# Two gated layers on one Trainium2 core: a sixth gate and up pair as seven block products, and an earlier panel split on ScalarE

## The reference, cut to what matters

```python
def _swiglu(h, w_in, w_out):
    gate, up = jnp.split(h @ w_in, 2, axis=-1)
    return (jax.nn.silu(gate) * up) @ w_out

x = x + _swiglu(_rmsnorm(x, norm2[i]), w_ffn_in[i], w_ffn_out[i])   # i = 0, 1
```

## Time and profile before

| what | value |
|---|---|
| median of 3 runs | 2103.74 us (2103.64 to 2107.66) |
| the profiled execution | 2107.25 us |
| its span in the profile | 2105.5 us, 40321 instructions |
| TensorE busy | 2025.5 us (96%) |
| VectorE busy | 1462.1 us (69%) |
| ScalarE busy | 946.5 us (45%) |
| GpSimd busy | 289.1 us (14%) |
| mean granted TensorE clock | 0.993 |
| DMA | 173.89 MB, mean 83 GB/s |

### The profile page before, as it was taken

The page is one execution under the profiler, slowest core; times in us unless marked ns, Lnnn a source line. Parts: engine busy times, 40 slices in busy tenths (PEclk is TensorE's granted clock), DMA queues, the critical chain, the costliest instruction groups (busy, mean ns, idle before and its releaser), DMA issues. The chain is left out here.

```text
span 2105.5 us, 40321 instructions
## 1 busy us (share of the span) xinstructions
PE 2025.5 (96%) x17186; PEld 1280.6 (61%) x17186; DVE 1462.1 (69%) x2207; ACT 946.5 (45%) x1459; POOL 289.1 (14%) x344
## 2 busy tenths in 40 slices
PE   7999999999999999999999999999998999999998
PEld 3657554565588444888745665885565445445766
DVE  4776764888799468765458887986746475786774
ACT  4335765433354674423244433645345345332433
POOL 2621331000001010222110000111012102000000
PEclk9999999999999999999999999999999999999999
DMA  6452003333434311010033333443410022332331
GB/s 159 129 146 56 2 2 87 94 102 99 115 102 123 101 61 60 16 51 4 3 89 90 103 105 110 129 118 101 139 62 21 21 81 60 101 100 65 116 116 65
DMA packets 259224, 173.89 MB, mean 83 GB/s; under 512 B 22528, under 2 KB 254148, under 8 KB 259044
## 3 DMA queue, kind: packets, MB, share of 16 engines
q1 hardware_dynamic: 258138, 170.35, 27.7%
q10 hardware_dynamic: 906, 0.96, 0.2%
HBM read 169.18 MB, written 2.10 MB: 81 GB/s over the span
## 5 line engine op out<-in xcount | busy, mean ns | idle before, releaser
L2718 DVE TENSOR_TENSOR w_lo<-wring,w_hi 128x2048 bf16<-128x2048 f32 (+5 forms) x258 | 440.4, 1718 | 180.6 <-ACT w_hi L2050 179.4
L1312 PE MATMUL banks<-arena,w_hi 128*128 128x512 bf16 (+3 forms) x1840 | 531.6, 372 | 6.4 <-issue 3.5
L2050 ACT ACTIVATE w_hi<-wring 128x2048 f16<-128x2048 f32 (+5 forms) x258 | 366.2, 1431 | 319.9 <-DVE wring L2711 150.0
L1312 PE MATMUL banks<-arena,w_lo 128*128 128x512 f16 (+1 forms) x920 | 342.4, 372 | 0.0
L1312 PEld LDWEIGHTS banks<-arena,w_hi 128*128 128x128 f16 x1840 | 179.8, 98 | 211.6 <-issue 10.6
L1388 PE MATMUL banks<-arena,w_hi 128*128 128x256 f16 (+1 forms) x1848 | 303.4, 273 | 4.3 <-ACT rcol L2099 2.7
L1388 PE MATMUL banks<-arena,w_lo 128*128 128x256 f16 x924 | 251.9, 273 | 0.0
L1150 POOL TENSOR_TENSOR arena<-arena,ntmp 128x512 f32<-128x512 f32 (+1 forms) x72 | 93.2, 1294 | 1108.4 <-ACT ntmp L2080 1102.4
L1312 PE MATMUL banks<-h_hi,w_hi 128*128 128x512 f16 (+1 forms) x536 | 204.0, 381 | 5.1 <-DVE w_lo L2718 5.1
L1312 PE MATMUL banks<-h_hi,w_lo 128*128 128x512 f16 (+1 forms) x536 | 203.9, 380 | 0.0
L1312 PE MATMUL banks<-h_lo,w_hi 128*128 128x512 bf16 (+1 forms) x536 | 203.7, 380 | 0.0
(11 more groups left out here) (479 smaller groups left out, 3395.5 us busy)
## 6 DMA issues: line engine op xcount, KB each, us to landing
wring<-in_w_ffn_in SPq DMA_DIRECT2D x68, 512.0 KB, 5.1
wring<-in_w_ffn_out SPq DMA_DIRECT2D x64, 256.0 KB, 4.0
wring<-in_w_ff SPq DMA_DIRECT2D x16, 1024.0 KB, 5.4
wring<-in_rw_w_in SPq DMA_DIRECT2D x11, 1024.0 KB, 5.3
wring<-in_w_in SPq DMA_DIRECT2D x11, 1024.0 KB, 5.2
wring<-in_w_ffn_in SPq DMA_DIRECT2D x40, 256.0 KB, 3.8
wring<-in_w_ff SPq DMA_DIRECT2D x32, 256.0 KB, 3.8
wring<-in_nsa_w_in SPq DMA_DIRECT2D x7, 1024.0 KB, 6.6
```

The costliest lines, as they stand in the source:

```text
L1312: last = mm(v, p[0], p[1], start=(i == 0), stop=(i == len(prods) - 1))
L2050: A(hi, raw, ACT.Copy).then_inc(split_hi, 1)
L2718: V.tensor_tensor(lo_, raw, hi, ALU.subtract).then_inc(split_lo, 1)
```

## The change

A sixth job of each gated layer, number 20, the 21st, becomes a block. TensorE, at the end of the job loop, waits for the last evacuation of the layer's blocks (all their second tiles), since what follows may use banks 4 to 7. ScalarE, in a job that is followed by a block (4, 7, 10, 13, 16, 19), makes the high halves up to the `split_ahead` of that block before the Silu of the job; that adds one panel, the plain one behind the block. VectorE's program order has no such edit.

```diff
-BLOCKED = (5, 8, 11, 14, 17)
+BLOCKED = (5, 8, 11, 14, 17, 20)
...
                     products(u_[0], u_[1])
+                read_out(pe, [st["ts"][1] for _, _, _, st, _ in jobs if st is not None])
                 if f is ffn[1]:
                     arrived(mem2_panel)
...
-                for g_, u_, e_, st, w in jobs:
+                for n, (g_, u_, e_, st, w) in enumerate(jobs):
                     t = g_[0]
                     split_to(split_ahead(w))
                     if st is not None:
...
                         A(term_t[:, 0:4:3, :], sets(bank[4]), ACT.Copy).then_inc(first_copied, 1)
+                    if e_ + 1 in BLOCKED:
+                        split_to(split_ahead(jobs[n + 1][4]))
                     act.wait_ge(evac_v, t.order + 1)
                     A(gate_b[e_ % 2], gate_b[e_ % 2], ACT.Silu).then_inc(silued, 1)
```

## The result

The changed kernel takes a median of **2112.52 us** (2110.98 to 2115.31, 6 runs); the kernel before, beside it on the same chip, 2103.51 (2102.17 to 2107.66, 6 runs). The ratio is 1.0041, with a 95% interval of 1.0030 to 1.0051: 9.0 us slower by the medians, 6.3 to 10.7 by the interval. The profiled execution of after took 2112.33 us, close to its median.

A forecast was written before the change was run, and what follows sets the result against it. TensorE was taken to bound the kernel, busy 2025.5 us, 96% of the span. 2 x 3.6 - 1.16 + 1.5 = +7.5 us on the median of 2103.74 gave 2111.2 us; range 2104.5 to 2115.

The forecast's parts named there:

- The block itself: TensorE's gated jobs: a block replaces a plain pair, -1.19 us per layer; the added wait behind the job loop costs nothing.
- The early split: ScalarE splits ahead of Silu, so TensorE's gap behind block 5 goes: -0.58 us per layer, -1.16 in all.
- the cover at odd jobs: Job 13: Silu's delay is hidden because VectorE waits for block 14 until 502.92 anyway, with 0.8 us to spare.
- What the block pushes: VectorE behind block 20: up 21 starts at +15.4 us, the second pair panel 14.5 behind job 21's products, before 9.73.
- +3.6 per layer: Second pair panel in the first layer, 1338.94 us in the second: +4.8 late less the block's 1.19, each layer.
- The clock: TensorE behind the first layer's second pair panel gap: slow stretch, +1.5 us; in the second layer nearly free.
- Rival 2: Slow stretches count in both layers, as second-layer splits wait for units TensorE reads late: +1.5 more, 2112.7 us; chance 0.1.
- rival 1: No slow clock behind either layer's gap: +6.0, 2109.8 us; chance 0.2.
- Rival 3: VectorE catches up, second pair panel's low half ready by 583.2: -3.5, 2100.2 us; chance 0.17.
- Rival 4: Early split delays Silu at odd jobs beyond its cover, blocks slip while VectorE catches up: 2104.4 us; chance 0.08.
- The sum: Whole kernel: 2 x 3.6 - 1.16 + 1.5 = +7.5 us; 2114.8 against the profiled execution, 2111.2 against the median.

The follow-up runs named there:

- the run with 18 filling products: Changed kernel plus 18 unused products of ones by ones ahead of the first layer's second pair panel wait: 2110.57 us, ratio 1.0026.
- the block alone: Changed kernel without ScalarE's early split, all six blocks kept: 2113.93 us, ratio 1.0045.
- the split alone: Changed kernel without the block at job 20, so five blocks with the early split: 2102.64 us, ratio 0.9985.
- the late sums: Changed kernel with the first pair panel's sums and their halves moved behind the pair's mixing in job 21: 2107.93 us, ratio 1.0016.
- the sixth block at 19: Changed kernel with blocks at 5, 8, 11, 13, 16 and 19, early split kept: 2101.64 us, ratio 0.9982.
- eight blocks: Changed kernel with blocks at every odd job from 5 to 19, early split kept: 2095.07 us, ratio 0.9956.
- seven blocks: Changed kernel with blocks at 5, 7, 9, 11, 13, 16 and 19, early split kept: 2097.59 us, ratio 0.9964.
- eight without the early split: Changed kernel with blocks at every odd job from 5 to 19 and ScalarE's early split removed: 2133.93 us, ratio 1.0141.

## Why the prediction was right

It forecast 2111.2 us and slower; measured were 2112.5 and slower. Step by step, in the prediction's order:

- **The block itself, 9.17 us and free read-out wait:** as predicted. No gap stands at 574.35.
- **The early split, -0.58 per layer:** the gap behind block 5 is gone in both layers. The term was set too small: the gap costs 0.70 per layer and not 0.58, since TensorE loses another 0.1 us before block 8, so -1.4 where -1.16 was counted. Alone, the split moves the root of the second layer from 1338.94 to 1337.37, by 1.57 us, of which 0.2 stand already at the start of block 5 (404.21, before 404.39), and the medians by 1.6. Of the cover at odd jobs, 0.8 us by the prediction, enough was left: TensorE has no gap in the gated jobs.
- **What the block pushes:** behind block 20 the next split of ScalarE starts at +4.60 (predicted 4.61), the plain unit's low half ends its wait and starts at +6.10 (6.12), up 21 at +15.37 (15.4), the second pair panel at +24.89, 14.53 behind job 21's products (14.5). TensorE's gap is 4.59 (near 4.9), gate 21 takes 0.43. The borrowed rows of block 14, an even block too, gave each of these within 0.1 us.
- **+3.6 per layer:** with the -0.58 the prediction has +3.0 per layer; the account shows -0.7 - 1.2 + 4.8 = +2.9 in the first and +2.9 in the second.
- **The clock, +1.5:** the stretch behind the first gap was at 0.70 and cost 1.67 us by the run with 18 filling products. In the second layer it was at 0.50, costlier for the products, and was absorbed before the root, as predicted: the chain took 34.22 us and not more. Rival 2 falls by this row, rival 1 by the first stretch. The size of the term owes something to luck all the same: the block alone, with the same gap of 4.58 in the first layer, had 0.50 and not 0.70 there, and the 1.00 behind the gap of 2.71 in the earlier trace rows, the prediction's only row for a gap of that length, was the exception among the kernels profiled (last section). The Trainium skill ("TensorE: Matmul & The Clock Gate", Part 1: The HAM clock gate) says that the throttled state is the default and activity releases it. The trace agrees, in a dense part of the kernel too: 0.70 and 0.50 behind gaps of 4.59 and 4.42.
- **Rival 3**, that VectorE catches up by 583.2: the low half ended at 588.7. **Rival 4**, that the early split slips blocks: the split alone is not slower.
- **The sum, +7.5:** the account up to the root of the second layer gives 8.5 - 1.0 = +7.5. The medians give +9.0, with 6.3 to 10.7 in the interval; 1.5 us are left, which these runs do not tell from the scatter between executions. The expected place of the remainder, a clock that differs from one execution to the next, is shown below in several kernels, but is not shown to be the cause of these 1.5. That the sum meets the trace to 0.1 us is in part luck: the split's term was 0.2 too small and the clock's 0.2 too small, and they have opposite signs.

One thing was set too loosely. The sum against the profiled execution (2114.8) and that against the median (2111.2) lay 3.6 us apart, and the prediction chose the median without saying why. The reason could have been looked for in the trace: the low clock between 1620 and 1640 us, worth 3.3 us, stands there and has nothing to do with the gated layers.

The added wait at the end of TensorE's job loop was not taken out in a run, as TensorE could then write a bank that is still being read; that it costs nothing rests on the trace alone.

## What to carry to other kernels

When work is made cheaper on the engine that bounds the kernel, follow the same edit through the queues of its feeders, up to the first chain without slack: here 1.19 us saved in products next to such a chain made it start 4.8 late in each layer, and with the last block one job earlier nothing was lost. An operation that waits for another engine belongs ahead of the ones that this engine has to wait for in turn; whether this matters is a question of spacing, 1.4 us with blocks three jobs apart and 39 with two. A neighbour of the same kind in the trace of before (another even block) predicts times in such queues to 0.1 us.

## What was not expected of the hardware

**The clock behind the same gap differs.** Eight of the kernels profiled wait 2.71 us at the root of the second layer. The granted clock over the 5.6 us behind it is in the earlier trace rows for before; the same stretch of five others follows, one fence for each (the split alone, the block alone, the late sums, the sixth block at 19, eight blocks):

```profile
1337.40:1343.00 5.60, 5.60 (x52) 5.03 (x53) 5.50 (x9) 1.29 (x1) 0.00 (x0) 1.00 0.57 190
```

```profile
1349.30:1354.90 5.60, 5.60 (x38) 4.44 (x39) 5.50 (x9) 1.32 (x1) 0.00 (x0) 0.72 0.58 189
```

```profile
1343.90:1349.50 5.60, 5.60 (x38) 4.47 (x39) 5.50 (x9) 1.32 (x1) 0.00 (x0) 0.73 0.59 189
```

```profile
1336.30:1341.90 5.60, 5.60 (x36) 4.32 (x37) 5.50 (x9) 1.32 (x1) 0.00 (x0) 0.70 0.56 189
```

```profile
1331.10:1336.70 5.60, 5.58 (x38) 4.41 (x39) 5.50 (x9) 1.34 (x1) 0.00 (x0) 0.72 0.55 187
```

The gap and the work around it are the same, and the clock was 1.00 twice and 0.70 to 0.73 in the six others, 0.70 with seven blocks and with eight without the early split too. The same holds for longer gaps: behind 4.42 to 4.43 us in the second layer the four kernels that have it show 0.50, 0.73, 0.70 and 0.60, and behind 4.58 us in the first layer the block alone had 0.50 where after had 0.70. So a slow stretch of 1.7 us is not a fixed price of a gap, and one profile cannot say which an execution will have. Whether the runs' spread (2098.36 to 2104.20 for the sixth block at 19) is made of such stretches stays open; only one execution of each kernel was profiled.

**Small float32 products are dear.** A product of 128 x 128 ones took 223 ns (28 of them, each two passes in the trace, from 583.16 to 589.41), as much as one of 512 columns in 16 bits (216 ns). With 18 of them as a filler the clock was 1.00 behind the wait, in the one execution profiled. What overshoots the wait lies on the path: 28 made TensorE 1.5 us late.
